# Convolution layers of a fused six-layer network: thirteen of sixteen z units behind the last value unit

## What is computed

```
D_MODEL = 1024; SEQ = 256; D_INNER = 2048; CONF_KERNEL = 31

def conformer_conv_mixer(h, w_in, conv_w, conv_b, ln_g, ln_b, w_out):
    proj = h @ w_in                                   # 256x1024 @ 1024x6144
    val, glu_gate, z = jnp.split(proj, 3, axis=-1)
    u = val * jax.nn.sigmoid(glu_gate)
    u = causal_depthwise_conv(u, conv_w) + conv_b     # 31 taps
    u = jax.nn.silu(layer_norm(u, ln_g, ln_b))        # over all 2048 channels
    return (u * jax.nn.silu(z)) @ w_out

hn = rms_norm(x, a_norm[j])
x = x + conformer_conv_mixer(hn, ...)
```

## Time and profile before

| | |
|---|---|
| median of three runs | 1800.94 us (1800.76 to 1802.33) |
| profiled execution, own time | 1800.72 us |
| its span, first to last instruction | 1798.9 us |
| PE busy | 1737.4 us, 97% |
| DVE busy | 1450.5 us, 81% |
| ACT busy | 1070.5 us, 60% |
| POOL busy | 309.5 us, 17% |
| mean granted TensorE clock | 0.99 |

### The profile page before, as it was taken

How to read it: one execution, slowest core, us unless ns; L and a number is a source line. 1 busy time by engine, 2 the same in 40 slices (tenths; PEclk the granted TensorE clock), 3 DMA queues, 4 the chain that set the end, 5 groups by cost and what they waited for, 6 DMA issues and landing times. The chain is left out here.

```text
span 1798.9 us, 30905 instructions
## 1 busy us (share of the span) xinstructions
PE 1737.4 (97%) x11610; PEld 1571.0 (87%) x11610; DVE 1450.5 (81%) x2731; ACT 1070.5 (60%) x2039; POOL 309.5 (17%) x396
## 2 busy tenths in 40 slices
PE   7998999999999999999989999999999999999996
PEld 6887788888889999988877989989999998999996
DVE  6999778887788888779987688788777788788666
ACT  6887665554454444478965556565555556575554
POOL 2998000000000000078940000003000200003000
PEclk9999999999999999999989999999999999999999
DMA  6454468855568888644445554546765444546551
GB/s 230 150 156 153 132 206 301 270 194 170 193 206 289 288 296 292 211 151 149 147 130 187 171 194 140 165 161 195 239 212 164 157 149 123 179 143 218 195 180 67
DMA packets 92741, 339.62 MB, mean 189 GB/s; under 512 B 10288, under 2 KB 10672, under 8 KB 91952
## 3 DMA queue, kind: packets, MB, share of 16 engines
q1 hardware_dynamic: 92592, 337.64, 56.7%
HBM read 336.55 MB, written 1.05 MB: 188 GB/s over the span
## 5 line engine op out<-in xcount | busy, mean ns | idle before, releaser
L103 PE MATMUL ps<-XS,wh 128*128 128x256 f32 x4464 | 828.0, 287 | 7.5 <-DVE wl L119 3.8
L103 PEld LDWEIGHTS ps<-XS,wh 128*128 128x128 f32 x4464 | 702.5, 193 | 27.7 <-issue 17.3
L119 DVE TENSOR_TENSOR wl<-raw,wh 128x1024 fp32r<-128x1024 f32 x481 | 589.4, 1252 | 104.3 <-ACT wh L112 103.2
L103 PE MATMUL ps<-XS,wl 128*128 128x256 f32 x2232 | 634.0, 284 | 0.0
L112 ACT CAST wh<-raw 128x1024 fp32r<-128x1024 f32 x481 | 487.1, 1045 | 151.0 <-PE ps L103 141.1
L103 PEld LDWEIGHTS ps<-XS,wl 128*128 128x128 f32 x2232 | 429.9, 193 | 0.1
L119 POOL TENSOR_TENSOR B<-B,tmp 128x236 f32<-128x236 f32 (+11 forms) x368 | 269.7, 774 | 649.9 <-ACT tmp L109 649.7
L103 PE MATMUL ps<-wh,os 128*128 128x512 f32 x864 | 284.4, 395 | 11.4 <-DVE os L119 6.8
L129 DVE SCALAR_TENSOR_TENSOR ps<-B,C,ps 128x253 f32<-128x253 f32 (+17 forms) x560 | 217.1, 466 | 9.3 <-ACT ps L109 9.3
L103 PEld LDWEIGHTS ps<-wh,os 128*128 128x128 f32 x864 | 163.1, 189 | 50.5 <-DVE os L119 11.1
L103 PE MATMUL ps<-B,raw 128*128 128x256 f32 x832 | 183.3, 380 | 0.8 <-ACT B L109 0.8
(11 more groups left out here) (161 smaller groups left out, 1616.6 us busy)
## 6 DMA issues: line engine op xcount, KB each, us to landing
raw<-in_w SPq DMA_DIRECT2D x628, 512.0 KB, 4.4
B<-in_ln SPq DMA_DIRECT2D x4, 1024.0 KB, 6.2
C<-in_cst SPq DMA_DIRECT2D x1, 1103.5 KB, 10.4
X<-in_x SPq DMA_DIRECT2D x2, 512.0 KB, 5.8
out_x<-X SPq DMA_DIRECT2D x4, 256.0 KB, 2.5
cb<-in_cb SPq DMA_DIRECT2D x1, 512.0 KB, 12.9
pos<-in_pos SPq DMA_DIRECT2D x1, 160.0 KB, 2.3
raw<-in_w SPq DMA_DIRECT2D x1, 128.0 KB, 2.9
```

The costliest lines, as they stand in the source:

```text
L103: return NOTHING if self.e is None else self.e.matmul(*a, **k)
L119: return NOTHING if self.e is None else self.e.tensor_tensor(o, a, b, op)
```

## The change

z units 0, 1 and 2 stay in the loop, behind value pairs 2, 4 and 6; the other thirteen come after value pair 7. The stream of pieces follows the same order. Only z pairs 0 and 1 still use bank 7; pairs 2 to 7 join the rotation of banks 4, 5 and 6. The sums of pairs 5, 6 and 7, the token sums and the spread stand at other places between the z units, and the casts, subtractions and Silus of ACT and DVE are moved to fit. The set of operations on PE, DVE and POOL is the same.

```
+EARLY_Z = (2, 4, 6)
 def plan_a(j):
     for p in range(8):
         two("g", p, E, "plain")
         two("v", p, 0, "split" if p else "plain")
-        if 1 <= p < 7:
-            out += z_unit(p - 1)
-    for x in range(6, 16):
+        if p in EARLY_Z:
+            out += z_unit(EARLY_Z.index(p))
+    for x in range(len(EARLY_Z), 16):
         out += z_unit(x)
 def a_order(self):
-        seq = [(kind, p) for p in range(8) for kind in "gv"] + [("z", p) for p in range(4, 8)]
+        seq = [(kind, p) for p in range(8) for kind in "gv"] + [("z", p) for p in range(2, 8)]
         bank = {x: 4 + i % 3 for i, x in enumerate(seq)}
         prior = {x: seq[i - 3] for i, x in enumerate(seq) if i >= 3}
-        for p in range(4):
-            bank["z", p] = 7
-            if p:
-                prior["z", p] = ("z", p - 1)
+        bank["z", 0] = bank["z", 1] = 7
+        prior["z", 1] = ("z", 0)
 def pe_a(self, pe, j):
-            if 1 <= p < 7:
-                pair("z", (p - 1) // 2, ((p - 1) % 2,))
-        pair("z", 3)
+            if p in EARLY_Z:
+                x = EARLY_Z.index(p)
+                pair("z", x // 2, (x % 2,))
+        pair("z", 1, (1,))
         stats(5)
+        pair("z", 2)
+        pair("z", 3, (0,))
+        stats(6)
+        pair("z", 3, (1,))
         pair("z", 4)
-        stats(6)
-        pair("z", 5)
-        pair("z", 6, (0,))
+        pair("z", 5, (0,))
         stats(7)
+        pair("z", 5, (1,))
         pe.wait_ge(*s["evac"][A, "S"])
...
-        pair("z", 6, (1,))
+        pair("z", 6)
         pe.wait_ge(*s["norm"][(A, "m"), "root"])
-        pe.wait_ge(*s["evac"][A, "z", 3])
+        pe.wait_ge(*s["evac"][A, "z", 1])
         self.spread(pe, 7, self.m["sm"][:, 112:116], (A, "m"))
         pair("z", 7)
 def act_a(self, act, j):
             if p == 7:
-                self.feed_act(act, f"{A}.z5.0", 0)
+                self.feed_act(act, f"{A}.z4.1", 0)
...
             else:
-                silu_z(3)
-                self.feed_act(act, f"{A}.z5.1", 0)
+                self.feed_act(act, f"{A}.z5.0", 0)
+                silu_z(1)
             items(p, 10, 14)
-            self.feed_act(act, f"{A}.v{p + 2}.0" if p < 6 else f"{A}.z{2 * p - 8}.0", 0)
-            if p in (2, 4, 6):
-                silu_z(p // 2 - 1)
+            if p < 6:
+                self.feed_act(act, f"{A}.v{p + 2}.0", 0)
+            if p == 4:
+                silu_z(0)
             items(p, 14, 18)
             if p:
                 stats(p - 1)
+            if p == 7:
+                self.feed_act(act, f"{A}.z5.1", 0)
             items(p, 18, 22)
             if p >= 6:
-                self.feed_act(act, f"{A}.z{2 * p - 8}.1", 0)
+                self.feed_act(act, f"{A}.z4.0" if p == 6 else f"{A}.z6.0", 0)
+            if p == 7:
+                silu_z(2)
             items(p, 22, 30)
+        silu_z(3)
+        self.feed_act(act, f"{A}.z6.1", 0)
+        stats(7)
         silu_z(4)
-        self.feed_act(act, f"{A}.z7.0", 0)
-        stats(7)
         act.wait_ge(*s["sums"][A, 7])
         ... copy "S" ...
+        self.feed_act(act, f"{A}.z7.0", 0)
         act.table(ACT.Sqrt)
 def dve_a(self, dve, j):
             if p == 7:
-                self.feed_dve(dve, f"{A}.z5.0", 0)
+                self.feed_dve(dve, f"{A}.z4.1", 0)
             items(p, 8, 14)
             if p == 7:
-                self.feed_dve(dve, f"{A}.z5.1", 0)
+                self.feed_dve(dve, f"{A}.z5.0", 0)
             items(p, 14, 20)
             if p < 7:
                 val(p + 1)
-            self.feed_dve(dve, f"{A}.v{p + 2}.0" if p < 6 else f"{A}.z{2 * p - 8}.0", 0)
+            if p < 6:
+                self.feed_dve(dve, f"{A}.v{p + 2}.0", 0)
+            if p == 7:
+                self.feed_dve(dve, f"{A}.z5.1", 0)
             items(p, 20, 28)
             if p >= 6:
-                self.feed_dve(dve, f"{A}.z{2 * p - 8}.1", 0)
+                self.feed_dve(dve, f"{A}.z4.0" if p == 6 else f"{A}.z6.0", 0)
             items(p, 28, 30)
         conv_end(7)
+        self.feed_dve(dve, f"{A}.z6.1", 0)
         self.feed_dve(dve, f"{A}.z7.0", 0)
```

## The result

The change makes the kernel slower. The median is 1822.97 us (1816.2 to 1829.06, four runs) against 1800.85 (1798.47 to 1802.33) of the kernel before beside it: a ratio of 1.0115 [1.0096, 1.0134]. The forecast was 1796.1. The profiled execution took 1823.07 us, its span 1821.2, which is 22.3 more than before. In the kernel after, helper lines have a number one higher (L104 for L103, L120 for L119).

A forecast was written before the change was run, and what follows sets the result against it. PE, busy 97%, was taken as full, with a0's loop at DVE's pace and a1's at PE's. a0 -2.0 + 1.3 = -0.7 and a1 -5.2 + 1.1 = -4.1 gave -4.8 us: 1796.1, range 1793.0 to 1801.0.

The forecast's parts named there:

- the pricing of the wl subtractions: DVE, both layers: subtractions taken at 1.20 us, some up to 1.67; making those fast could gain 1.5 us more a layer.
- D: Rival, chance 0.07: clock falls for two stretches at each new PE wait in the loop, delaying DVE; 1803 to 1806.
- The loop's gain: Convolution loops up to the last value pair: 2.0 us earlier in a0 and 5.2 in a1.
- The ACT waits of DVE: DVE's waits in the loop for ACT's first tap of a pair, 2.0 us in a0 and 4.6 in a1, would go.
- V: The end of value pair 7 on PE, from which tail times count: 145.47 in a0, 892.54 in a1 before the change.
- The tail: From V to the spread: 39.4 us against 38.1 and 38.3, so longer by 1.3 us in a0 and 1.1 in a1.
- V to sums 6: Tail: PE's work ends at V + 14.6, then it waits 1.4 us for ACT's squares, where it waited 3.45.
- Sums 7: Tail: PE at V + 28.9 waits 0.5 us, as conv_end(7) and the squares are ready at V + 29.4.
- rival B: Chance 0.25: another wait leaves half the loop's gain, -1.2 us, or tail clock falls, -2.4; 1798 to 1800.
- The clock: PE: sum assumes 1.00 throughout; new loop waits of about 2, 3.7 and 3.2 us a layer may bring falls to 0.50.
- the cover: Loop: DVE takes up a value pair 2.2 us after PE ends it, covering 1.7 us of delay but not 3.4.

The follow-up runs named there:

- POOL's holds: Changed kernel, but POOL waits before certain adds until a DVE wl subtraction is done: 1800.52 us, ratio 0.9992 to the kernel before.
- the kernel before with the same holds: Kernel before the change, with POOL waiting before certain adds for DVE's wl subtractions: 1799.83 us, ratio 0.9989 to the kernel before.
- the kernels without the network: Network left out; DVE makes k PSUM operations, then one subtraction, beside POOL's 36 adds (236 columns; then 100, 236, 480): held subtraction 15.22 us at k = 21.

## Why the prediction was wrong, point by point

**The step that failed** is the pricing of the wl subtractions. The prediction put them at 1.20 to 1.67 us as in the earlier trace rows, for a loss as for a gain, and took POOL's idle time (3.05 us in the earlier trace rows, beside the casts' 2.32 and 2.29 in the earlier trace rows) for pure waste. It was part of what let DVE's subtractions in. By removing it the change gave POOL unbroken runs, and three subtractions took 7.89, 11.86 and 8.12 us. None of the rivals had this; D forecast a slowdown, by another mechanism and a tenth of the size. The experiments settle it: breaking the runs removes the loss, taking a pause out of the kernel before makes one.

**The loop's gain** was there under the loss. The ACT waits of DVE fell as said, from 2.0 to 0.4 us in a0 and from 4.6 to none in a1. With POOL's holds V in a0 came at 144.99, 0.5 earlier, or 1.1 if counted from POOL's first add (33.72 there, 33.12 before); forecast 2.0. Two subtractions of that loop still took 2.70 and 2.00 us, 2.3 more than at 1.2 each, which may be what is missing. From the spread of a0 (185.20) to V in a1 (888.59) 5.6 us were gained; forecast 5.2. (The 887.3 that the prediction gives for V in a1 leaves out a0's 0.7; by its own sum it is 886.6. With the holds it was 888.59.)

**The tail** was mis-sized. V to sums 6 without PE's wait is 14.7 us, forecast 14.6. The wait was 2.51 and 2.53 us, forecast 1.4; what makes the squares 1.1 us later is open, and moving the cast of z5.0 did not shorten it. Sums 7 found no wait, forecast 0.5, though `conv_end(7)` waited 2.45 us for POOL, whose last adds came later than the prediction had them. In a0 the clock fell behind sums 6 (0.53 from 168 to 170), and the stretch to sums 7 took 14.5 us instead of 12.9; in a1 it stayed at 1.00. With the holds the tail is 40.2 and 40.0 us, so +2.1 and +1.7 instead of +1.3 and +1.1.

So without held subtractions the terms make -0.5 + 2.1 - 5.6 + 1.7 = -2.3 us in place of -4.8: rival B's amount, though B had it from another wait in the loop and from the clock in the tail. The profiled execution with the holds shows it (its span is 2.0 us shorter than before), but that was one of the quicker of 11: their median is 1.2 us below the kernel before beside it, with an interval that includes no change, and 0.7 above the kernel before with the same holds. A gain of the new order by itself is not shown.

**The clock** did fall in the loop after the new waits, as rival D and the section "HAM oscillation — how this bites in real kernels" of the Trainium skill's "TensorE: Matmul & The Clock Gate" had it. PE had stood 5.11 us until 59.88 and 3.62 until 128.47. Two windows of the kernel after (PE, PEld, DVE, ACT, POOL busy, clock, DMA):

```profile
58.90:65.70 6.80, 5.82 (x26) 5.76 (x27) 6.80 (x17) 4.23 (x11) 5.98 (x10) 0.50 0.27 77
127.10:133.90 6.80, 5.43 (x25) 5.46 (x26) 6.80 (x16) 5.73 (x14) 6.80 (x10) 0.50 0.27 77
```

DVE is busy all through both: it is the bound. Behind the first pair it waited only 0.24 us for PE in all of a0's loop, so the cover held over two stretches, for which rival D had reckoned 1.2 us at each of three places. In a1 the loop's loss is explained without the clock: 10.7 + 6.9 - 5.6 is 12.0, and 11.9 was measured.

## What to carry to other kernels

Before removing a wait of an engine that is off the critical path, ask what gets in during it; a pause of GpSimd can be what lets VectorE's two-input SBUF operations run. When busy time grows at an unchanged number of instructions, group by tile and read the maximum, not the mean: three instructions in 481 made this loss. Before a cast or a load is moved, look up which piece its buffer held before, and when that one is done. If GpSimd makes long runs of SBUF operations beside such an operation of VectorE, let it wait for that operation at a fixed place: here it cost nothing.

## What the runs showed of the hardware

A long run of POOL's adds with inputs ready holds a DVE subtraction with two SBUF inputs out until the run ends or POOL stops for a moment. In the kernels without the network, a subtraction that came up to about the end of the 14th add got in when the add under way was done (1.2 to 2.2 us in all); one that came later did not. It is a number of adds and not a time (4.75, 8.41 and 15.75 us into the run for the last short one). Adds from before a pause of 1.27 us did not count, and a subtraction with one input in PSUM was not held in any of five trials. By the rule of the page of the Trainium skill named above a wait of one add was to be expected; a subtraction of up to 25.94 us was measured, and the measurement decides.

In the network a long run alone is not enough. The 82 adds of the earlier trace rows have subtractions of 1.20 and 1.67 us in them. The traces of the network kernels without holds, read add by add, separate long from short by two things together. The first is the number of adds begun since DVE last got in or POOL last stood still: each subtraction that gets in delays one add, to about 1.7 us, and the count seems to start again with it. With up to 11 adds all were short, some of them with the next product ready for 1.3 to 1.6 us; the eleven held ones came with 13 or 16. So 14 is the number of the small kernel and not exactly that of the network. The second is that POOL's next product had been ready for over 1 us (1.11 to 1.63) when the current add began; with 13 to 18 adds but the next product ready for 0.9 us or less, all were short. Both were read from traces and not tried by themselves in the network; nor is it known what sets the limit.
